# Up projection: convolution accumulator in PSUM banks 6 and 7, order of the token sums and of the first GELU, two low halves on VectorE

## What is computed

```
up = h @ w_up                                  # 1024 -> 2 x 2816 features
a, g = split(up, 2)
g = conv3x3_depthwise(g as rows x cols) + b_dw # latent: 16 x 64 grid, context: 1 x 128
y = (gelu(g) * a) @ w_down                     # 2816 -> 1024
x = layer_norm(ALPHA * x + g2 * y)
```

## Time and profile before

| what | value |
|---|---|
| median of three runs | 1469.07 us (1468.04 to 1473.06) |
| the execution profiled | 1468.26 us, span 1466.5 us, mean granted clock 0.96 |
| TensorE busy | 1318.1 us, 90% |
| VectorE busy | 1113.7 us, 76% |
| POOL busy | 663.3 us, 45% |
| ScalarE busy | 580.8 us, 40% |
| HBM read and written | 142.88 and 27.80 MB, 116 GB/s over the span |

### The profile page before, as it was taken

How to read it: one execution, slowest core, us unless ns; L and a number is a source line. 1 busy time by engine, 2 the same in 40 slices (tenths; PEclk the granted TensorE clock), 3 DMA queues, 4 the chain that set the end, 5 groups by cost and what they waited for, 6 DMA issues and landing times.

```text
span 1466.5 us, 22280 instructions
## 1 busy us (share of the span) xinstructions
PE 1318.1 (90%) x7871; PEld 1213.1 (83%) x7871; DVE 1113.7 (76%) x1455; ACT 580.8 (40%) x977; POOL 663.3 (45%) x433
## 2 busy tenths in 40 slices
PE   5898999789986999966899999898999989999996
PEld 3688999789986778966898989898999978888784
DVE  7556579464576887797999999999978975764856
ACT  5532234334355345513333333343434445343440
POOL 1004997313441212257777777777768760000000
PEclk9899999989998999987999999999999999999998
DMA  9432213542333531201222222131312168385571
GB/s 333 130 98 68 84 58 116 161 133 77 104 111 128 186 115 58 65 22 52 90 68 80 76 70 86 52 104 52 104 45 91 58 217 305 123 277 177 192 261 56
DMA packets 150411, 171.65 MB, mean 117 GB/s; under 512 B 9831, under 2 KB 109507, under 8 KB 150083
## 3 DMA queue, kind: packets, MB, share of 16 engines
q1 hardware_dynamic: 149854, 165.93, 35.4%
q0 software_dynamic: 288, 4.72, 0.8%
q10 hardware_dynamic: 197, 0.06, 0.0%
HBM read 142.88 MB, written 27.80 MB: 116 GB/s over the span
## 4 chain that ended last, share of the span: by engine, by line
PE 42%; DVE 6%; issue 6%; POOL 2%; ACT 1%; POOLq 0%; DVEq 0%; ACTq 0%
PE ps L1307 9%; PE ps L1309 8%; PE ps L1308 8%; PE ps L1335 5%; PE ps L1337 5%; PE ps L1336 5%; DVE acc L2645 3%; POOL wsum L2077 1%; DVE zt L2741 0%; DVE zb L2739 0%; POOL tlo L1868 0%; POOL xlo L1868 0%; DVE acc L2648 0%; DVE taps L2656 0%; POOL wlo L1868 0%
## 5 line engine op out<-in xcount | busy, mean ns | idle before, releaser
L2645 DVE SCALAR_TENSOR_TENSOR acc<-gs,taps,acc 128x945 f32<-128x945 f32 (+2 forms) x176 | 323.8, 1840 | 33.8 <-ACT acc L1719 28.4
L2016 POOL TENSOR_TENSOR rstd<-mv,neghalf 128x1 f32<-128x1 f32 x27 | 25.2, 932 | 336.8 <-DVE mv L2533 328.7
L965 PE MATMUL ps<-h1hi,whi 128*128 128x384 f32 x432 | 154.9, 359 | 0.0
L965 PE MATMUL ps<-h1lo,whi 128*128 128x384 f32 x432 | 147.4, 341 | 0.0
L965 PE MATMUL ps<-h1hi,wlo 128*128 128x384 f32 x432 | 147.4, 341 | 0.0
L1868 POOL TENSOR_TENSOR wlo<-raw,whi 128x512 fp32r<-128x512 f32 x50 | 84.5, 1693 | 85.9 <-ACT whi L1738 34.1
L1307 PE MATMUL ps<-thi,xhi 128*128 128x288 f32 x320 | 97.2, 304 | 20.2 <-issue 16.9
L1307 PE MATMUL ps<-thi,whi 128*128 128x288 f32 x320 | 96.8, 303 | 16.5 <-issue 16.5
L1309 PE MATMUL ps<-thi,wlo 128*128 128x288 f32 x320 | 96.5, 302 | 0.0
L1308 PE MATMUL ps<-tlo,whi 128*128 128x288 f32 x320 | 96.4, 301 | 0.0
L1309 PE MATMUL ps<-thi,xlo 128*128 128x288 f32 x320 | 96.3, 301 | 0.0
(11 more groups left out here) (401 smaller groups left out, 4174.7 us busy)
## 6 DMA issues: line engine op xcount, KB each, us to landing
raw<-in_w_down SPq DMA_DIRECT2D x132, 256.0 KB, 3.4
raw<-in_w_up SPq DMA_DIRECT2D x78, 256.0 KB, 3.5
u_rows<-acc SPq DMA_DIRECT2D x22, 576.0 KB, 3.0
ur<-u_rows SPq DMA_DIRECT2D x66, 192.0 KB, 3.6
adaw<-in_w_ada SPq DMA_DIRECT2D x24, 512.0 KB, 4.0
raw<-in_w_in SPq DMA_DIRECT2D x40, 256.0 KB, 4.2
adaw<-in_w_ada SPq DMA_DIRECT2D x8, 1024.0 KB, 10.4
Dm<-scan_rows SPq DMA_DIRECT2D x18, 256.0 KB, 4.7
```

Source lines behind the costliest of these rows:

```text
L965: last = mm(ps[:, bank, 0:GN], a[:, n % 2, k * P:(k + 1) * P], b[:, kk, grp(g)], start=(kk == 0 and a is whi and b is h1hi), stop=(kk == K ...
L2016: tt(rstd[:, j % 4, :], mv[:, j % 4, 1:2], neghalf[:, 0, :], ALU.pow).then_inc(rstd_ready, 1)
L2645: step(stt(a3[:, ro, co], g3[:, ri, ci], taps[:, tap:tap + 1], a3[:, ro, co], ALU.mult, ALU.add), 2 + m)
```

## The change

The part of the convolution accumulator that belongs to the latent tokens becomes banks 6 and 7 of PSUM (`acc_lat`), with one buffer; the 128 context tokens get a small buffer of their own in SBUF (`acc_ctx`). `acc_init`, `gelu` and `u_make` become two instructions each. u is written to a new pair of buffers `ub`, from which the store goes. `acc_init` now waits for u_ready of the tile before, and `u_make` for the store of two tiles before. What used bank 7 in the last body goes to the columns from 288 on of bank 0, between products 4 and 5 of the first and third tile. The banks of the down projection shift by two. In the code before the loop ScalarE rounds token sums 1 and 3 earlier and takes weight blocks 0 and 1 around the first GELU; `acc_init(1)` moves to the end. The low halves of token sums 3 and 2 are both VectorE's, and `t_lo(3)` leaves POOL.

Small edits left out: the placing of `acc_ctx` and `ub`, call sites of `gelu` and `u_make` whose arguments changed, and views of `gs` in `conv`.

```diff
@@ -336,6 +337,9 @@
         ps = stack.enter_context(nc.psum_tensor("ps", [P, 8, 512], F32))
+
+        acc_lat = ps[:, 6:8, :].rearrange("p a n -> p (a n)")
+        AUX = TC
@@ -457,7 +461,7 @@
         def down_bank(g, i):
-            return (2 * GT * g + i + 6) % 8
+            return (2 * GT * g + i) % 8
@@ -1294,10 +1298,12 @@
                         pe.wait_ge(c22_added, j + (C_0 + done))
-                    if n in (1, 2, 6):
-                        pe.wait_ge(tlo_pool, L_0 + {1: 1, 2: 2, 6: 3}[n])
-                    elif n == 4:
-                        pe.wait_ge(tlo_dve, L_0 + 1)
+                    if n in (1, 2):
+                        pe.wait_ge(tlo_pool, L_0 + n)
+                    elif n in (4, 6):
+                        pe.wait_ge(tlo_dve, L_0 + 2)
+                    if aux is not None and n == 5:
+                        aux()
                     hi_w, lo_w = xslot(N_PROD * jj + n)
@@ -1314,16 +1320,24 @@
                     seven(b, jj)
-            pe.wait_ge(ada3_used, 1 + N_ADA3 * KT)
-            for j in range(N_ADA3):
-                last = acc_cols(7, 2 * j * AB, aacc2[j])
-            last.then_inc(pe_ada, 1)
+            def ada3_cols():
+                pe.wait_ge(g_out, FT - N_BODY + 1)
+                pe.wait_ge(ada3_used, 1 + N_ADA3 * KT)
+                for j in range(N_ADA3):
+                    last = acc_cols(0, AUX + 2 * j * AB, aacc2[j])
+                last.then_inc(pe_ada, 1)
+
+            def gate_rows2():
+                pe.wait_ge(g_out, FT - N_BODY + 3)
+                nc.tensor.transpose(ps[0:2 * KT, 0, AUX:AUX + P], adaT[:, A_G2:A_G2 + KT, :].rearrange("p k w -> p (k w)"),
+                                    ident[:, :]).then_inc(pe_grows, 1)
+
             for jj in range(N_BODY):
-                if jj == N_BODY - 2:
+                if jj == 1:
                     pe.wait_ge(ada_b, 2)
-                    nc.tensor.transpose(ps[0:2 * KT, 7, 0:P], adaT[:, A_G2:A_G2 + KT, :].rearrange("p k w -> p (k w)"),
-                                        ident[:, :]).then_inc(pe_grows, 1)
-                seven(BODIES - 1, jj)
+                if jj == 3:
+                    pe.wait_ge(growT_ready, 3)
+                seven(BODIES - 1, jj, {0: ada3_cols, 2: gate_rows2}.get(jj))
@@ -1341,10 +1355,7 @@
                     for i in range(GT):
-                        if i == 1:
-                            pe.wait_ge(g_out, FT)
-                        if i == 2:
-                            pe.wait_ge(val_copied, V_0 + FT)
+                        pe.wait_ge(*((g_out, FT), (val_copied, V_0 + FT), (c12_added, A_0 + FT - N_PLAIN))[i])
                         for r in range(4):
@@ -1361,6 +1372,8 @@
                                 pe.wait_ge(down_used, GT * g + i - 3)
+                            elif r < 2 and GT * g + i == 3:
+                                pe.wait_ge(u_ready, FT)
                             last = down_mms(g, i, r % 2, kt0 + r // 2, n0 + r, r < 2, False)
@@ -1710,13 +1723,17 @@
-            def gelu(i, par):
+            def gelu(i):
                 act.wait_ge(conv_ready, i + 1)
-                fn(acc[:, par, :], acc[:, par, :], ACT.Gelu_apprx_tanh, bias=taps[:, NTAP:NTAP + 1]).then_inc(gelu_ready, 1)
+                bias = taps[:, NTAP:NTAP + 1]
+                fn(acc_ctx[:, :], acc_ctx[:, :], ACT.Gelu_apprx_tanh, bias=bias)
+                fn(acc_lat, acc_lat, ACT.Gelu_apprx_tanh, bias=bias).then_inc(gelu_ready, 1)
...
                 act.wait_ge(conv_step, N_STEP * i + 1)
-                fn(acc[:, par, :], gs[:, par, :], ACT.Copy, scale=taps[:, 4:5]).then_inc(acc_begun, 1)
+                act.wait_ge(u_ready, i)
+                fn(acc_ctx[:, :], gs[:, par, LAT:T], ACT.Copy, scale=taps[:, 4:5])
+                fn(acc_lat, gs[:, par, 0:LAT], ACT.Copy, scale=taps[:, 4:5]).then_inc(acc_begun, 1)
@@ -1788,8 +1805,9 @@
                     next_hi(b, jj, 2)
+                if aux is not None:
+                    aux()
                 act.wait_ge(c12_added, j + (A_0 + jj + 1))
-                act.wait_ge(u_out[par], 8 * j + (UO_0 + 16 * ((N_PLAIN + jj) // 2)))
                 acc_init(j + (N_PLAIN + jj), par)
@@ -1807,30 +1825,32 @@
+            t_hi(1)
...
+            t_hi(3)
...
-            t_hi(1)
...
-            gelu(0, 0)
+            act.wait_ge(pe_unit, U_S - 1)
+            s_hi(0, 0, 0)
+            gelu(0)
+            act.wait_ge(pe_unit, U_S)
+            s_hi(0, 0, 1)
+            fn(wide(val[:, 1, :]), ps[:, 3:6, 0:GN], ACT.Copy).then_inc(val_copied, 1)
+            for n in range(2, 4):
+                s_hi(0, 0, n)
+            t_hi(2)
...
-            t_hi(3)
-            act.wait_ge(pe_unit, U_S - 1)
-            s_hi(0, 0, 0)
-            act.wait_ge(pe_unit, U_S)
-            fn(wide(val[:, 1, :]), ps[:, 3:6, 0:GN], ACT.Copy).then_inc(val_copied, 1)
-            for n in range(1, 4):
-                s_hi(0, 0, n)
-            t_hi(2)
...
+            def grow_evac():
+                act.wait_ge(pe_grows, 3)
+                fn(growT2[:, :], ps[0:2 * KT, 0, AUX:AUX + P], ACT.Copy).then_inc(growT_ready, 1)
+
...
-                if jj == N_BODY - 1:
-                    act.wait_ge(pe_grows, 3)
-                    fn(growT2[:, :], ps[0:2 * KT, 7, 0:P], ACT.Copy).then_inc(growT_ready, 1)
-                seven(BODIES - 1, jj, jj == N_BODY - 1)
+                seven(BODIES - 1, jj, jj == N_BODY - 1, grow_evac if jj == 2 else None)
@@ -2102,15 +2122,7 @@
             t_lo(1)
-            s_sum(0, 0, 0)
-            s_low(0, 0, 0)
-            s_sum(0, 0, 1)
-            s_low(0, 0, 1)
-            t_lo(3)
-            s_sum(0, 0, 2)
-            s_low(0, 0, 2)
-            s_sum(0, 0, 3)
-            s_low(0, 0, 3)
+            ahead(0, 0)
             with pool.Fori(0, BODIES - 1) as b:
@@ -2645,8 +2658,7 @@
                     co, ci = shifted(CTX, dx)
-                    ins = stt(a_all[:, LAT:T][:, co], g_all[:, LAT:T][:, ci], taps[:, 4 + dx:5 + dx], a_all[:, LAT:T][:, co],
-                              ALU.mult, ALU.add)
+                    ins = stt(acc_ctx[:, co], g_ctx[:, ci], taps[:, 4 + dx:5 + dx], acc_ctx[:, co], ALU.mult, ALU.add)
                     if dx < 0:
@@ -2656,10 +2668,13 @@
-            def u_make(i, par):
+            def u_make(i, par, stored):
                 dve.wait_ge(gelu_ready, i + 1)
                 dve.wait_ge(val_copied, i + (V_0 + 1))
-                tt(acc[:, par, :], acc[:, par, :], val[:, par, :], ALU.mult).then_inc(u_ready, 1)
+                if stored is not None:
+                    dve.wait_ge(u_out[par], stored)
+                tt(ub[:, par, LAT:T], acc_ctx[:, :], val[:, par, LAT:T], ALU.mult)
+                tt(ub[:, par, 0:LAT], acc_lat, val[:, par, 0:LAT], ALU.mult).then_inc(u_ready, 1)
@@ -2687,7 +2702,7 @@
                 tt(c22, c22, ps[:, PB:PB + 2, 0:TC], ALU.add).then_inc(c22_added, 1)
-                u_make(j + (N_PLAIN + jj - 1), 1 - par)
+                u_make(j + (N_PLAIN + jj - 1), 1 - par, 8 * j + (UO_0 + 16 * ((N_PLAIN + jj - 1) // 2)))
                 load_taps(i)
@@ -2700,10 +2715,11 @@
             t_sum(2)
-            u_make(0, 0)
+            u_make(0, 0, None)
             load_taps(1)
-            dve.wait_ge(thi_ready, T_0 + 4)
-            tt(tlo[:, 2, :, :], tf[:, 2, :, :], thi[:, 2, :, :].bitcast(F32), ALU.subtract).then_inc(tlo_dve, 1)
+            for q in (3, 2):
+                dve.wait_ge(thi_ready, T_0 + T_ORDER.index(q) + 1)
+                tt(tlo[:, q, :, :], tf[:, q, :, :], thi[:, q, :, :].bitcast(F32), ALU.subtract).then_inc(tlo_dve, 1)
             dve.wait_ge(pe_unit, U_S)
@@ -2717,7 +2733,7 @@
                     dve.wait_ge(pe_ada, N_ADA1 + N_ADA2 + 1)
-                    tt(adaT[:, A_G2:6 * KT, :], ps[:, 7, 0:2 * KT].rearrange("p (b w) -> p b w", w=2),
+                    tt(adaT[:, A_G2:6 * KT, :], ps[:, 0, AUX:AUX + 2 * KT].rearrange("p (b w) -> p b w", w=2),
                        bc(colv[:, V_BADA + A_G2:V_BADA + 6 * KT].unsqueeze(2), [P, KT, 2]), ALU.add).then_inc(ada_b, 1)
```

More of the change, by code:

```diff
@@ L153, in layer @@
         wgr = place("wgr", [P, KT, NGATE])
+        acc_ctx = place("acc_ctx", [P, CTX], top[0] - 4 * KT * NGATE)
         wg2 = place("wg2", [P, KT, G2], dt=F32R)
@@ L246, in layer @@
         gs = place("gs", [P, 2, T])
-        acc = place("acc", [P, 2, T])
+        ub = place("ub", [P, 2, T])
         val = place("val", [P, 2, T])
@@ L706, in store_u @@
                 sp.wait_ge(u_ready, count)
-                sp.dma_start(u_rows[bass.ds(P * i, P), :], acc[:, par, :]).then_inc(u_out[par], 16)
+                sp.dma_start(u_rows[bass.ds(P * i, P), :], ub[:, par, :]).then_inc(u_out[par], 16)
             def up_loads(b, jj, blk=None):
@@ L1277, in plain_tile, with seven @@
                     last.then_inc(pe_unit, 1)
-            def seven(b, jj):
+            def seven(b, jj, aux=None):
                 j, done = N_BODY * b, jj + 1
@@ L1758, in us_hi, with seven @@
```

(13 more changed lines are left out.)

## The result

The changed kernel takes 1406.15 us (median of four runs, 1404.67 to 1409.17), the one before 1469.08: a ratio of 0.957 with a 95% interval of 0.954 to 0.960, 62.9 us less. I had forecast 1417 and a range of 1408 to 1444. The direction and the mechanism hold; the gain is 11 us larger than the likeliest value and 2 us outside the range.

The account below looks back on a forecast made before the run. VectorE was taken to set the pace of the sixteen tiles that carry ada3. Gains of 14 (beginning), 37 (loop) and 1 (seam), 52 off 1468.26 us, gave 1416, plus a microsecond for the edges: 1417 us, range 1408 to 1444.

Parts of the forecast that it names:

- VectorE sets the pace through the addition for product 6: Looped tiles with ada3: TensorE waits for all of VectorE's work of a tile, 24.6 us summed against 24.87 seen.
- TensorE needs 22.2 us a tile: Looped tiles: 168 matmuls at 0.132 us each, the pace expected once TensorE's waits go.
- rival of another wait that takes over: ScalarE's queue or a last-four-tiles wait replaces TensorE's: 1 us in each of 19 tiles, 1436; within partial gain's 0.24.
- A tap costs 1.22 us: VectorE's latent convolution taps with the accumulator in PSUM: eight cost 9.8 us instead of 14.45.
- 1.45 to 1.7: Rival of a partial gain: PSUM taps cost this many us, at 1.6 a tile takes 23.4, kernel 1434; chance 0.24.
- POOL's delay kept: Rival: taps stay at 1.81 us since gs still comes from SBUF, kernel 1464; chance 0.05.
- two cycles an element: Slower rival: taps reading and writing PSUM in place take turns, always 2.1 us, kernel 1518; chance 0.09.
- The beginning: Ahead of the first looped tile's product 6: start at 682.7 to 692 instead of 701.24, 9 to 18 us gained.
- The loop: 40 less 3 for a clock that stays low: Fifteen looped tiles at TensorE's pace give 40 us, less about 3 of half speed after the restart: 37.
- The last four tiles, left at nothing: Moving ada3's column products, gate transpose and copy to bank 0 there costs nothing, at most 1 us.
- the seam, 1: At the down projection's seam TensorE's 3.77 us wait for POOL's us1lo gets about 1 us shorter.
- A microsecond back for the edges: Whole kernel: one microsecond added to the summed 1416 us, giving 1417.

Follow-up runs that it names:

- extra5: The changed kernel with five extra zero-weight taps over the whole latent grid in every convolution; 1448.51 us (0.986).
- extra6: The changed kernel with six extra zero-weight taps over the whole latent grid in every convolution; 1475.89 us (1.006).
- pair2: The changed kernel with two extra zero-weight VectorE operations per convolution, both inputs in SBUF, output in the u buffer; 1435.75 us (0.978).
- psum_only: The changed kernel with the old order ahead of the loop, low half of sum 3 on POOL; 1411.73 us (0.961).
- extra2: The changed kernel with two extra zero-weight taps over the whole latent grid in every convolution; 1411.46 us (0.960).

## Why the prediction was wrong in size and right in kind

- *VectorE sets the pace through the addition for product 6* and *TensorE needs 22.2 us a tile*: right. The loop now runs at 22.26, and only extra5, extra6 and pair2, which fill VectorE's time, bring the waits back. The rival of another wait that takes over falls too, since TensorE has no wait there.
- *A tap costs 1.22 us*: right, median 1.215. The three rivals that rest on a dearer tap (1.45 to 1.7; POOL's delay kept; two cycles an element) fall with this one row. The Trainium skill (VectorE: DVE Perf Modes, the section on the TRN2 errata) gives 120 fixed cycles for a source in PSUM against 58 for one in SBUF. The difference does not show here: 945 elements take 1.206 us with the source in PSUM and 1.20 at their shortest with both inputs in SBUF, 1008 elements 1.272 and 1.27. The 0.75 us of line 2689, which the forecast set against it, could not have settled it, since no row had 576 elements with both inputs in SBUF.
- *The beginning: "I take 14"*: this is the step that failed. The chain worked out from rows gave 18.5 us; the profile has 19.6. I replaced it by a value near the middle of 9 to 18, where 9 stood for every SBUF pair held by POOL. The chain itself was 1.1 us too long: measured were 0.9 and 0.74 us for the context taps of convolutions 0 and 1 against 1.6 and 2.15, 2.6 for u_make and the copies against 2.9, but 9.7 for sum 2 against 8.7. Error 5.6 us, of which 4.5 are the step from 18.5 to 14.
- *The loop: 40 less 3 for a clock that stays low*: right, 36.5. A tile of 22.26 instead of 22.2 takes 0.9 of the 40, and the first tile after the restart loses 2.5 us at half speed. 0.5 us too much was taken.
- *The last four tiles, left at nothing, and the seam, 1*: 1.9 and 2.6. Of the 1.9, 1.7 is the shorter fall of the clock in the tile with the column products; as its length differs between executions of one kernel, I call it luck. At the seam the wait shrank by 1.5 us, to 2.27, and a wait of 0.8 us ahead of the first matmuls there is gone. Error 3.5 us.
- *"A microsecond back for the edges"*: nothing in the rows stood for it. Error 0.7.
- These errors, 5.6 - 0.5 + 3.5 + 0.7 = 9.3 us, make 60.6 out of 51.3. The spans of the profiles differ by 1.5 less, since the part ahead of the change took that much longer in the one after; the medians differ by 62.9, and the 2.3 beyond 60.6 lie within what the part ahead varies by.
- *The range* began at 1408, although 18 + 40 + 1 from the bounds of the very text gives 1409 without any of the variation between executions: its lower end was the sum of the terms' own best cases. The loop stayed within its bounds, but the beginning (19.6 against 18), the last four tiles (1.9 against nothing) and the seam (2.6 against 1) went beyond theirs.
- *VectorE's tile of 20.4 us*: too high by 2.1. I left the context taps, the context part of gate times value and the tap copy as slow as before. In the changed kernel these cost 0.35, 0.29 and 0.16 us, while ada3's operations went up from 0.88 to 1.27. It changed nothing in the time, since TensorE has the bound, but it made the slack look like 1.8 us instead of 4.0, and with it the rival of a partial gain too likely.
- *One buffer, the moved columns, the banks of the down projection, ScalarE's second instructions*: nothing, as said. The idle time for the start of the accumulator is 29.1 / 18 = 1.6, 1.67 expected.

Not tried: the accumulator with one buffer and the second instructions, but in SBUF. So psum_only's 57.5 us are those of all these edits together; that the place is what counts among them rests on the durations of the taps and on pair2. What VectorE's own shorter instructions and what POOL's shorter ones contribute is not separated either.

## What to carry to other kernels

When an engine's instruction has two durations in a profile, one of them its work and the other its work plus an operation of a neighbour, look for an operand that can move to the other memory, before looking for fewer instructions: here the same 176 taps became 33% shorter (mean 1.84 to 1.23 us). And once a chain has been added up from rows, keep that sum as the value and let the held case be the range's end; the retreat toward that end, 4.5 us, was the largest single part of this forecast's error of 10.9. Last, where effects of 2 to 4 us are compared, take the falls of the clock out of the windows first: one tile alone differed by 1.6 us between two executions of one kernel.

## What was unexpected of the hardware

- Pauses of TensorE of 1.6 to 1.9 us in every tile of 24.2 us (extra5; the first pause there is 0.4) went with a granted clock of 1.00 in the tiles with ada3. Pauses of 1.4 to 3.2 us in tiles of 25.4 (extra6) went with falls to 0.5 every second or third tile, pauses of 0.6 to 2.75 before with falls every third or fourth. In extra6 each of these falls stood right behind a pause of 2.9 us or more, but one of 3.0 passed without a fall, and so did one of 2.75 before. What separates them is not settled by these runs.
- A fall needs no pause: eleven of the twelve profiles have one behind or among the 32 two-column matmuls of the column products, with TensorE busy throughout (27.28 us of 27.28 in the changed kernel's window).
- A fall of the clock is free in a stretch paced by another engine, since the pause behind it shrinks by the same 1.5 us. Where TensorE sets the pace, 3.4 us of half speed cost 1.5 us and 6.8 us cost 3.1 (the tile with the column products, 25.8, 27.3 and 28.95 us).
- POOL's delay lands on whichever VectorE instruction with two SBUF inputs comes next, however short, and moves when anything around it shifts: in extra2, with nothing but PSUM taps added, ada3's two rose by 0.47 us each, and in pair2 the 127-element taps took 1.26 us instead of 0.35.
- Two SBUF inputs are not the only case. The copy of nine tap weights has one input, in SBUF, and it took 1.24 to 1.27 us in 20 of 22 runs before, each while POOL computed, and at most 0.17 after. The rows before and after:

```profile
L2656 DVE COPY taps<-dwc x22: 165/1256/1271, 611.0 to 1172.1; 128x9 f32 x16, 128x9 f32<-128x9 f32 x6
```

```profile
L2668 DVE COPY taps<-dwc x22: 155/161/167, 612.5 to 1112.8; 128x9 f32 x16, 128x9 f32<-128x9 f32 x6
```
